# A one-core encoder kernel: 24 transposes and an earlier Silu at the first expert; a new order of loads, fp32 blocks and final normalisation at the last

## The reference, cut to what matters

```
gate, idx = top_k(softmax(u @ router_w).T, 64)      # 64 rows of each sequence to each expert
xs  = u[idx]
hid = silu(xs @ w_gate[e]) * (xs @ w_up[e])         # 1024 -> 2048
out = hid @ w_down[e] * gate                        # 2048 -> 1024
h   = h + scatter_add(out, idx)
y   = rmsnorm(h, g_fin)
```

## Time and profile before

| | us |
|---|---|
| runs without the profiler, median of 3 | 1658.25 (1657.61 to 1658.35) |
| the profiled execution, its own time | 1658.02 |
| its span, first to last instruction | 1656.2 |
| PE busy | 1585.8 (96%) |
| DVE busy | 1279.7 (77%) |
| ACT busy | 1050.1 (63%) |
| POOL busy | 119.0 (7%) |

### The profile page before, as it was taken

How to read it: one execution, slowest core, us unless ns; L and a number is a source line. 1 busy time by engine, 2 the same in 40 slices (tenths; PEclk the granted TensorE clock), 3 DMA queues, 4 the chain that set the end, 5 groups by cost and what they waited for, 6 DMA issues and landing times.

```text
span 1656.2 us, 22461 instructions
## 1 busy us (share of the span) xinstructions
PE 1585.8 (96%) x8198; PEld 1319.7 (80%) x8198; DVE 1279.7 (77%) x1266; ACT 1050.1 (63%) x941; POOL 119.0 (7%) x65
## 2 busy tenths in 40 slices
PE   6999999999993999999999999999999999999993
PEld 5888888888882788888888888888888888888882
DVE  6474475564466788888898888888898888888886
ACT  4443355443343677777777777777777777777774
POOL 0000003000003001011010010110101101011011
PEclk9999999999995999999999999999999999999997
DMA  9342235443254899999999999999999999999993
GB/s 360 123 127 102 95 131 201 146 150 100 75 173 145 284 356 388 390 397 367 391 388 388 392 371 392 389 382 390 373 397 390 370 398 380 387 393 375 392 394 139
DMA packets 150326, 496.14 MB, mean 300 GB/s; under 512 B 9488, under 2 KB 34192, under 8 KB 150288
## 3 DMA queue, kind: packets, MB, share of 16 engines
q1 hardware_dynamic: 138848, 454.20, 72.7%
q0 software_dynamic: 10160, 38.28, 7.1%
q10 hardware_dynamic: 1280, 3.15, 0.7%
HBM read 471.47 MB, written 20.97 MB: 297 GB/s over the span
## 4 chain that ended last, share of the span: by engine, by line
PE 90%; DVE 4%; DMA 2%; ACT 2%; issue 1%; SPq 0%; ACTq 0%; DVEq 0%; POOL 0%; POOLq 0%
PE ps L1176 81%; PE ps L1250 2%; PE ps L1281 2%; PE ps L1471 2%; PE ps L1259 2%; PE ps L1440 1%; DMA arena<-h_rows 1%; DVE w_rest L796 1%; PE ps L1384 1%; DMA h_rows<-xh,rows 1%; DMA raw<-w_qkv 1%; PE ps L1373 0%; DVE arena L855 0%; DVE topi L1074 0%; DVE ut_rest L923 0%
## 5 line engine op out<-in xcount | busy, mean ns | idle before, releaser
L796 DVE TENSOR_TENSOR w_rest<-raw,w_high 128x2048 fp32r<-128x2048 f32 x224 | 510.3, 2290 | 97.9 <-ACT w_high L729 64.7
L729 ACT CAST w_high<-raw 128x2048 fp32r<-128x2048 f32 x188 | 360.1, 1915 | 138.3 <-PE ps L1176 138.3
L1176 PE MATMUL ps<-w_high,xt_high 128*128 128x512 f32 x1040 | 324.9, 394 | 2.1 <-DVE xt_rest L1138 1.0
L1176 PE MATMUL ps<-w_rest,xt_high 128*128 128x512 f32 x1040 | 321.3, 390 | 0.0
L1176 PE MATMUL ps<-w_high,xt_rest 128*128 128x512 f32 x1040 | 321.1, 390 | 0.0
L796 DVE TENSOR_TENSOR w_rest<-raw_more,w_high 128x2048 fp32r<-128x2048 f32 x96 | 218.6, 2290 | 49.2 <-ACT w_high L729 49.2
L796 DVE TENSOR_TENSOR w_rest<-early,w_high 128x2048 fp32r<-128x2048 f32 x96 | 218.5, 2289 | 23.0 <-ACT w_high L729 21.5
L1176 PEld LDWEIGHTS ps<-w_rest,xt_high 128*128 128x128 f32 x1040 | 195.8, 188 | 41.2
L1176 PEld LDWEIGHTS ps<-w_high,xt_rest 128*128 128x128 f32 x1040 | 195.8, 188 | 41.0
L729 ACT CAST w_high<-raw_more 128x2048 fp32r<-128x2048 f32 x96 | 184.0, 1917 | 69.8 <-PE ps L1176 69.8
L1176 PEld LDWEIGHTS ps<-w_high,xt_high 128*128 128x128 f32 x1040 | 193.7, 189 | 41.5 <-DVE xt_rest L1138 1.4
(11 more groups left out here) (164 smaller groups left out, 1930.4 us busy)
## 6 DMA issues: line engine op xcount, KB each, us to landing
raw<-w_gate SPq DMA_DIRECT2D x64, 1024.0 KB, 7.5
raw<-w_up SPq DMA_DIRECT2D x64, 1024.0 KB, 8.2
raw<-w_down SPq DMA_DIRECT2D x64, 1024.0 KB, 7.2
raw_more<-w_gate SPq DMA_DIRECT2D x32, 1024.0 KB, 7.8
raw_more<-w_up SPq DMA_DIRECT2D x32, 1024.0 KB, 8.3
early<-w_gate SPq DMA_DIRECT2D x32, 1024.0 KB, 8.0
early<-w_up SPq DMA_DIRECT2D x32, 1024.0 KB, 8.0
raw_more<-w_down SPq DMA_DIRECT2D x32, 1024.0 KB, 7.6
```

The lines of the kernel that those rows point to most:

```text
L729: nc.scalar.copy(w_high[:, i % SLOTS, :], raws[i % RAW_SLOTS]).then_inc(high_done, 1)
L796: nc.vector.tensor_tensor(w_rest[:, j, :], raws[j if r is None else r], w_high[:, j, :].bitcast(F32), ALU.subtract).then_inc(rest_done, 1)
L1176: done = nc.tensor.matmul(out, lhs, rhs, start=start and part == 0, stop=stop and part == 2)
```

## The change

At the first expert: PE gets 24 transposes of the identity into bank 2 ahead of `rows_t(0)`; nothing reads them. ACT's first Silu stands after 2 instead of 3 rounded pairs of the next half, and DVE's `step_hidden(0)` likewise.

At the last expert: SP waits for the scatter of expert 14 after the load of pair 11, and then issues, on its one queue, tiles 0 to 3 of `h_rows` in two DMAs of 1 MB, pairs 12 and 13, tiles 4 to 7 in two DMAs, pairs 14 and 15. POOL issues only the gather of `last_h`. Silu and hidden step stand one pair earlier. Pairs 14 and 15 are no longer split: ACT copies bank 7 (hidden columns 512 to 1023, transposed) as fp32 into `whole`, and PE multiplies it with the raw pairs, 8 fp32 matmuls of 128x512 in place of 24 fp32r ones. Only bank 6 is still split, for pairs 12 and 13.

At the final norm: DVE squares tile 1 in place of tile 6, and finishes all eight tiles; ACT loads the table of the root ahead of the squares of tiles 2 and 3. The addition of the last expert stands behind `finish(5)`. POOL computes nothing, and it no longer awaits its last scatter: SP does, on `y_last`.

```diff
 AHEAD = 3
-FIN_POOL = (2, 3)
-FIN_SQUARE = 6
-FIN_VECTOR = tuple(t for t in range(TRUNKS * TILES) if t not in FIN_POOL)
+FIN_TILES = TRUNKS * TILES
+FIN_SQUARE = 1
+WHOLE_PAIRS = (14, 15)
+        whole = silu[:, 0:BANK]
-        h_in = [sem(f"h_in{c}") for c in range(TRUNKS)]
...
                 load_run(e, 2 * GU_PAIRS + D_PAIRS, down_rows, e, 1, D_PAIRS)
             load_run(E - 1, 0, gate_up_rows, E - 1, 1, GU_PAIRS)
             load_run(E - 1, GU_PAIRS, down_rows, E - 1, 0, D_PAIRS)
-            load_run(E - 1, GU_PAIRS + D_PAIRS, down_rows, E - 1, 1, D_PAIRS)
-
-
-
-            for n, t in enumerate(FIN_VECTOR):
-                sp.wait_ge(fin_done, n + 1)
+
+            sp.wait_ge(scattered, 16 * (E - 1))
+            for c in range(TRUNKS):
+                for n in (2 * c, 2 * c + 1):
+                    i = 2 * (n % 2)
+                    sp.dma_start(h_rows[c][:, i:i + 2, :], h_dram[2 * n * P:2 * (n + 1) * P, :].rearrange("(i p) d -> p i d", p=P)).then_inc(h_in[n], 16)
+                for jj in (2 * c, 2 * c + 1):
+                    load_pair(E - 1, GU_PAIRS + D_PAIRS + jj, down_rows(E - 1, 1, jj))
+
+            for t in range(FIN_TILES):
+                sp.wait_ge(fin_done, t + 1)
                 sp.dma_start(y[t * P:(t + 1) * P, :], h_rows[t // TILES][:, t % TILES, :]).then_inc(y_out, 16)
-            sp.wait_ge(y_out, 16 * len(FIN_VECTOR))
+            sp.wait_ge(y_out, 16 * FIN_TILES)
+            sp.wait_ge(y_last, 16)
 
...
             last_rows = bass.IndirectOffsetOnAxis(ap=rows[:, E - 1:E], axis=0)
-            for c in range(TRUNKS):
-                out, src = rows_of(h_rows[c], h_dram, c)
-                pool.dma_start(out, src).then_inc(h_in[c], 16)
             pool.indirect_dma_start(last_h, None, h_dram, last_rows).then_inc(last_in, 16)
-            pool.wait_ge(grow_in, 16 * 2)
-            for n, t in enumerate(FIN_POOL):
-                pool.wait_ge(fin_scaled, n + 1)
-                row = h_rows[t // TILES][:, t % TILES, :]
-                nc.gpsimd.tensor_tensor(row, row, grow[:, :], ALU.mult).then_inc(fin_pool, 1)
-                pool.wait_ge(fin_pool, n + 1)
-                pool.dma_start(y[t * P:(t + 1) * P, :], row).then_inc(y_pool, 16)
-
-            pool.wait_ge(y_pool, 16 * len(FIN_POOL))
-            pool.wait_ge(y_out, 16 * len(FIN_VECTOR))
+
+            pool.wait_ge(y_out, 16 * FIN_TILES)
             pool.wait_ge(last_done, 1)
-            pool.indirect_dma_start(y, last_rows, last_h, None).then_inc(y_pool, 16)
-            pool.wait_ge(y_pool, 16 * (len(FIN_POOL) + 1))
+            pool.indirect_dma_start(y, last_rows, last_h, None).then_inc(y_last, 16)
...
             rows_high(0)
             highs(None, SLOTS, GU_PAIRS)
-            highs(0, 0, AHEAD)
+            highs(0, 0, 2)
             step_silu(0, GU_PAIRS - 1)
-            highs(0, AHEAD, HT_AFTER)
+            highs(0, 2, HT_AFTER)
             hidden_high(0)
...
-            highs(E - 1, HT_AFTER, 12)
-            step_silu(2 * E - 1, pairs_before(E - 1) + GU_PAIRS)
+            highs(E - 1, HT_AFTER, 11)
+            step_silu(2 * E - 1, pairs_before(E - 1) + GU_PAIRS - 1)
+            highs(E - 1, 11, 13)
 
...
             def h_square(t):
 
-                c, i = t // TILES, t % TILES
+                act.wait_ge(h_in[t // 2], 16)
                 n = t - (t > FIN_SQUARE)
-                act.wait_ge(h_in[c], 16)
                 if n >= 2:
                     act.wait_ge(ssq_f, n - 1)
-                square(4 + c, h_rows[c], i, (xg, ys)[n % 2], ssq_f)
-
-            def scale(n, t):
-                c, i = t // TILES, t % TILES
-                act.wait_ge(rstd_f, c + 1)
-                nc.scalar.activation(h_rows[c][:, i, :], h_rows[c][:, i, :], ACT.Copy,
-                                     scale=rstd[:, TILES * (4 + c) + i:TILES * (4 + c) + i + 1]).then_inc(fin_scaled, 1)
-
-            highs(E - 1, 12, 13)
+                square(4 + t // TILES, h_rows[t // TILES], t % TILES, (xg, ys)[n % 2], ssq_f)
+
             h_square(0)
+            act.wait_ge(ht_mm, 2 * E)
+            nc.scalar.copy(xt_high[:, 0:BANK], bank(6)).then_inc(hth_done, 1)
+            nc.scalar.copy(whole, bank(7)).then_inc(whole_done, 1)
             highs(E - 1, 13, 14)
-            h_square(1)
-            act.wait_ge(ht_mm, 2 * E)
-            nc.scalar.copy(xt_high[:, :], bank(6, 2)).then_inc(hth_done, 1)
-            h_square(2)
-            highs(E - 1, 14, 15)
-            h_square(3)
-            highs(E - 1, 15, 16)
+            nc.scalar.preload_act_table(ACT.Sqrt)
+            for t in range(FIN_SQUARE + 1, TILES):
+                h_square(t)
             root(4)
-            h_square(4)
-            for n, t in enumerate(FIN_POOL):
-                scale(n, t)
-            h_square(5)
-            h_square(7)
+            for t in range(TILES, FIN_TILES):
+                h_square(t)
             root(5)
 
             act.wait_ge(h_done, 1)
-            act.wait_ge(ssq_f, TRUNKS * TILES - 1)
+            act.wait_ge(ssq_f, FIN_TILES - 1)
             nc.scalar.activation(xg, last_h, ACT.Square, accum_out=ssq[:, 24:25]).then_inc(ssq_l, 1)
             root(6)
...
             rests(None, SLOTS, GU_PAIRS)
-            rests(0, 0, AHEAD)
+            rests(0, 0, 2)
             step_hidden(0)
+            rests(0, 2, AHEAD)
...
             rests(E - 1, AHEAD, HT_AFTER)
             hidden_rest(2 * E - 2)
-            rests(E - 1, HT_AFTER, 12)
+            rests(E - 1, HT_AFTER, 11)
+            dve.wait_ge(pair_used, pairs_before(E - 1) + GU_PAIRS)
             step_hidden(2 * E - 1)
-            rests(E - 1, 12, 14)
+            rests(E - 1, 11, 13)
             dve.wait_ge(hth_done, 2 * E)
-            nc.vector.tensor_tensor(xt_rest[:, :], bank(6, 2), xt_high[:, :].bitcast(F32), ALU.subtract).then_inc(htr_done, 1)
-            rests(E - 1, 14, 15)
-            one_over_rms(4)
-            rests(E - 1, 15, 16)
+            nc.vector.tensor_tensor(xt_rest[:, 0:BANK], bank(6), xt_high[:, 0:BANK].bitcast(F32), ALU.subtract).then_inc(htr_done, 1)
+            rests(E - 1, 13, 14)
             dve.wait_ge(grow_in, 16 * 2)
 
             def finish(t):
                 normalise(4 + t // TILES, h_rows[t // TILES], h_rows[t // TILES], t % TILES, fin_done)
 
-            finish(0)
-            finish(1)
-            dve.wait_ge(h_in[1], 16)
+            dve.wait_ge(h_in[FIN_SQUARE // 2], 16)
             at = TILES * 4 + FIN_SQUARE
-            part = h_rows[1][:, FIN_SQUARE % TILES, :]
+            part = h_rows[0][:, FIN_SQUARE, :]
             nc.vector.tensor_tensor_reduce(out=hid, in0=part, in1=part, scale=1.0, scalar=0.0, op0=ALU.mult, op1=ALU.add,
-                                           accum_out=ssq[:, at:at + 1]).then_inc(ssq_fd, 1)
-
+                                           accum_out=ssq[:, at:at + 1]).then_inc(ssq_d, 1)
+            one_over_rms(4)
+            for t in range(TILES):
+                finish(t)
+            one_over_rms(5)
+            for t in range(TILES, FIN_TILES - 2):
+                finish(t)
             dve.wait_ge(last_in, 16)
             dve.wait_ge(pair_used, pairs_before(E - 1) + GU_PAIRS + 2 * D_PAIRS)
             nc.vector.scalar_tensor_tensor(out=last_h, in0=bank(4, 2), scalar=gate_w[:, E - 1:E], in1=last_h,
                                            op0=ALU.mult, op1=ALU.add).then_inc(h_done, 1)
-            one_over_rms(5)
-            finish(4)
+            finish(FIN_TILES - 2)
+            finish(FIN_TILES - 1)
             one_over_rms(6)
-            finish(5)
-            finish(6)
-            finish(7)
             nc.vector.scalar_tensor_tensor(out=last_h, in0=last_h, scalar=rstd[:, 24:25], in1=grow[:, :],
                                            op0=ALU.mult, op1=ALU.mult).then_inc(last_done, 1)
 
...
+            for _ in range(24):
+                nc.tensor.transpose(bank(2)[:, 0:P], ident[:, :], ident[:, :])
             rows_t(0, None)
...
             hidden_t(2 * E - 1)
             down(2 * E - 2, 0, at(0), 8, 2, 4)
-            down(2 * E - 1, 1, at(0), 12, lhs=(xt_high, xt_rest))
+            down(2 * E - 1, 1, at(0), 12, 0, 2, lhs=(xt_high, xt_rest))
+            pe.wait_ge(whole_done, 1)
+            for i in WHOLE_PAIRS:
+                r = i % RAW_SLOTS
+
+                pe.wait_ge(raw_in[r], 16 * (body_turn(E - 1, i) + 1))
+                for k in range(2):
+                    c = 2 * (i - 12) + k
+                    for n in range(2):
+                        last = nc.tensor.matmul(bank(4 + n), whole[:, (c - 4) * P:(c - 3) * P],
+                                                raws[r][:, k * D + n * BANK:k * D + (n + 1) * BANK], start=False, stop=c == 7)
+                last.then_inc(pair_used, 1)
```

14 lines of the change are left out of this document (7 added, 7 removed).

## The result

The changed kernel takes **1640.9 us** (median of 4 runs, 1640.35 to 1641.75) against 1658.3 of the kernel before (4 runs, 1657.61 to 1658.48) on the same chip: ratio 0.9896, 95% interval [0.9884, 0.9908]. The forecast was 1639.1, in a range of 1636 to 1646. The profiled execution took 1640.4 us, its span is 1638.2.

A forecast was written before the change was run, and what follows sets the result against it. The loop over experts was taken as PE's alone, with gains only before and behind it: 1.0 + 1.5 + 1.7 + 12.3 + 2.4 = 18.9 us, span 1637.3, time 1639.1 us, range 1636 to 1646.

The forecast's parts named there:

- Warm-up: First expert on PE: 24 added transposes raise the clock before the first products; 1.0 us won, ends 0 and 2.0.
- Silu: First expert: the earlier Silu and hidden step let the hidden transposes start sooner after PE's last pair; 1.5 us won.
- Clock behind the gap: First expert: PE's idle before the hidden transposes shrinks to 1.2 us, so the clock is kept; 1.7 us won, ends 0 and 1.8.
- Pair 12 just hidden: Last expert: pair 12 lands at 1608.4, its rounding would start at 1608.7; the new wait is hidden by half a microsecond.
- The first rival: Last expert: pair 12 lands late, 6.2 us after ACT wants it; time 1645.3, chance 0.2.
- Last expert: From expert 14's scatter to POOL's last scatter: the chain on ACT and DVE ends 12.3 us sooner, bounds 9 and 13.
- fp32 products: PE's end: 8 fp32 products at 0.45 us each, 3.6 us; PE done at 1626.7, 2.1 us before DVE asks.
- The third rival: PE's end: fp32 products four times as dear, 7.3 us, so the addition waits for PE; 1640.7 us, chance 0.12.
- Drain: End of the program: POOL's drain lies beside the last scatter's transfer; 2.4 us won, or 0 if the drain waits.
- The second rival: Clock and drain give nothing: transposes don't warm PE, second start stays cold, drain waits; 1644.2 us, chance 0.2.
- The fourth: Last expert: the eight loads of the end don't overlap, so the kernel is slower than before; 1666.8 us, chance 0.02.

The follow-up runs named there:

- e2: The changed kernel with the first Silu and first hidden step back behind three rounded pairs; 1644.13 us, ratio 0.9916.
- e4: The changed kernel with POOL again awaiting its last scatter, in place of SP; 1642.34 us, ratio 0.9906.
- e9: The changed kernel with pairs 12 to 15 all split (no fp32 products) and queued ahead of the four h pieces; 1644.23 us, ratio 0.9917.
- e6: The changed kernel with POOL multiplying two tiles of dead data while DVE finishes tiles 0 to 3; 1645.49 us, ratio 0.9917.
- e8: The kernel before with only the edits at the first expert, 24 transposes and the earlier Silu and hidden step; 1654.06 us, ratio 0.9975.
- e10: The kernel before with POOL's two output tiles given to DVE, nothing else changed; 1656.40 us, ratio 0.9988.
- e5: The changed kernel with pairs 14 and 15 split again, so no fp32 products, loads still alternated; 1648.70 us, ratio 0.9941.
- e7: The changed kernel with the last expert's addition on DVE behind finish 6 instead of finish 5; 1640.22 us, again 1640.23, ratios 0.9888 and 0.9892.

## Why the prediction was right, and where it was not

The forecast came out 1.8 us low in the time and 0.9 in the span: 18.9 us of gain said, 18.0 found. Step by step:

- **Warm-up, 1.0 (0 to 2.0).** Right in kind; the sum took the middle. The changed kernel's profiles show the whole 2.0 (25.45 = 28.81 less 2.0 and less 1.4 for the Silu). Of the 11 profiles with the 24 transposes 7 show warm first products, 3 lost 1.5 to 1.6 us of it (e2, e4, e9), and e6 started cold. The middle was low for the commonest case and fair as a mean.
- **Silu, 1.5.** Measured 1.4 (idle 2.75 to 1.32).
- **Clock behind the gap, 1.7.** Found, 1.66 (e8); of the 1.85 from the first to the last hidden transposes 0.19 are the last half's earlier Silu. The clock stayed full behind the 1.32 us idle in all eleven profiles that have it. Behind 2.75 us it fell in the kernel before and in e10, but not in e2, so the gain isn't the code's alone.
- **Pair 12 just hidden, by half a microsecond.** Right: ACT took it behind PE at 1604.20, and that is no more than a hair, since in e5 the same load came 0.24 us late (an idle of 1.04 where PE's own wait is 0.80). The first rival was not far off in its place, but the pieces of `arena` took 4.8 and 7.6 us and not the 14.1 of before, as the argument against it had it.
- **Last expert, 12.3.** Measured 10.66; this is the term that failed, by 1.6. Against its own chain, the four finishes ended 0.35 us later than written and the next two 0.45: small change, 0.35 of it there when ACT took pair 12 (1609.05 in the forecast's times, 1608.7 written). The other 1.22 us is the addition's wait for PE.
- **fp32 products, 0.45 us each, PE done 2.1 us before DVE asks.** This step was wrong. They take 0.88 each, 7.03 in all. PE was done at 1625.54, in the forecast's times (later by 4.85 us, the last hidden transposes' 1611.58 less 1606.73) 1630.4, where it wrote 1626.7. The third rival, at 0.12, was the true mechanism: it had PE done at 1630.4 and a time of 1640.7; measured, 1640.9. That its time came so close is partly luck: the stretches gained 18.4 us to its 17.3, 1.0 of it by the warm-up, and a start 0.37 later and a median 0.5 above the profiled execution took that back. Its page, the Trainium skill's "FP8 and Floating Point Precision", section TensorE Precision Notes, gives true FP32 four passes: 4 x 0.227 = 0.91 by it, 0.88 measured, where the row of the 64x256 product had seemed to speak against it.
- **Why that row misled.** The earlier trace rows has 376 ns for a record, and I read it as a product. After the change 8 products leave 16 records of 0.59 us, so a record is no product. The score step behind the earlier trace rows issues 4 products and leaves 8 records in the timeline of PE before:

```profile
446.61 1.13 PE L1250 MATMUL ps<-early 64*128 64x256 f32 x8
447.68 0.39 PE L1176 MATMUL ps<-w_high,ut_high 128*128 128x256 f32 x1
447.90 0.28 PE L1176 MATMUL ps<-w_rest,ut_high 128*128 128x256 f32 x1
448.02 0.28 PE L1176 MATMUL ps<-w_high,ut_rest 128*128 128x256 f32 x1
```

  From 446.61 to 447.68 that is 1.07 us, 0.27 a product of 256 columns, over twice the 0.12 of an fp32r product (447.90 to 448.02). The four stand on alternating halves of 64 rows; if two of them run side by side, a pair takes 0.53, near the 0.48 of four fp32r products, and the row says much the same as the page. That they do wasn't tried.
- **Drain, 2.4.** Measured 2.5, and e4 takes 2.2 of it back. It does lie beside the transfer.

The second rival (clock and drain give nothing) is out in the profile for all three of its parts, though e2, e4, e6 and e9 show that the warm-up can fail in a single execution. The fourth, the eight loads one by one, is out: 420 GB/s throughout.

What made the gain of the end, then: no POOL tiles 1.66 (e10) to 2.9 (e6), and fp32 blocks 3.2 (e9 less the changed kernel), in which PE's late products, worth 1.09 in e7, are already counted. The rest, 10.66 less 3.2 less the 1.66 to 2.9, is 4.6 to 5.8 us: the new order of the end, with `arena` in time (14 us of the chain before were its read), DVE's square and both squares before the root early, one table load off the path. By place, from the last hidden transposes to the first finish it took 16.44 us before, 13.47 in e9 and 8.98 in the changed kernel; from there to the scatter 20.21, 15.70 and 17.01. So the fp32 blocks win 4.5 ahead of the first finish and lose 1.3 behind it, and of what isn't theirs 3.0 lie ahead of it and 4.5 behind, POOL's tiles included. These parts weren't run apart, so how the order's share divides is open.

## What to carry to other kernels

Count what a precision costs from a row whose products and records you have both counted: here the fp32 product was four fp32r products, and it still paid, since each pair left whole spares ACT a rounding of 1.9 us and DVE a subtraction of 2.3, and their chain ended last. An engine that helps another at its last elementwise tiles must be charged for what it slows: POOL's two tiles cost DVE more than doing them. Whether the order of the last loads matters depends on who asks for them: behind ACT's rounding it was worth 4.9 us, behind PE's own late products nothing, since the wait for them took up the 0.33 us that were lost. And to judge a microsecond, measure between two rows of the same engine chain; the span carries 1.8 us of start and up to 2.4 of clock at the first products (e6 against the changed kernel) that change from one execution to the next.
